# A three-block kernel whose mLSTM rows are spread over the partitions by DMA in place of picking matmuls

## The reference

```python
def mlstm_chunkwise(q, k, v, li, lf):
    ...
        m_row = jnp.maximum(inter, jnp.max(dmat, axis=-1))
        w_intra = jnp.exp(dmat - m_row[..., None])
        ...
        s_qk = jnp.einsum('bhld,bhsd->bhls', qj, kj) * w_intra
        num = jnp.einsum('bhls,bhse->bhle', s_qk, vj) + ...
        hj = num / jnp.maximum(jnp.abs(den), jnp.exp(-m_row))[..., None]
    ...
    hm = hm * jax.nn.sigmoid(heads(p['ml_o'], ML_HEADS))
    y_ml = rmsnorm(hm, ml_norm_g.reshape(ML_HEADS, ML_HD)).reshape(b, s, ML_W) * jax.nn.silu(p['ml_z'])
```

## Time and profile before

| | |
|---|---|
| median of 3 runs | 2338.71 us |
| lowest and highest run | 2337.97 and 2342.67 us |
| span of the profiled execution, first to last instruction | 2341.0 us |
| the profiled execution's own time | not given apart from the span |
| TensorE busy | 96% of the span |
| DVE, ScalarE, POOL busy | 51%, 40%, 38% |
| granted clock of TensorE, mean | 0.992 |
| DMA engines, mean busy share | 22.5% by the main queue |

### The profile page before, as it was taken

How to read it: one execution, slowest core, us unless ns; L and a number is a source line. 1 busy time by engine, 2 the same in 40 slices (tenths; PEclk the granted TensorE clock), 3 DMA queues, 4 the chain that set the end, 5 groups by cost and what they waited for, 6 DMA issues and landing times. The chain is left out here.

```text
span 2341.0 us, 38427 instructions
## 1 busy us (share of the span) xinstructions
PE 2245.5 (96%) x16046; PEld 1743.2 (74%) x16046; DVE 1193.9 (51%) x2014; ACT 947.8 (40%) x1364; POOL 898.2 (38%) x678
## 2 busy tenths in 40 slices
PE   7999999999999999999999988878999999999997
PEld 5776777787877857777788777776666778888885
DVE  5544834334245467342343878854644657317334
ACT  5423355345353324654343433324266342222243
POOL 4342343334434404333344422222333445545543
PEclk9999999999999999999999989999999999999998
DMA  4221221222222202222233200002211232232332
GB/s 159 84 85 36 73 90 64 72 73 85 98 81 81 90 22 87 81 66 79 68 106 104 72 3 4 4 19 77 72 64 57 81 105 91 99 99 91 99 99 72
DMA packets 50568, 175.18 MB, mean 75 GB/s; under 512 B 6036, under 2 KB 7004, under 8 KB 50396
## 3 DMA queue, kind: packets, MB, share of 16 engines
q1 hardware_dynamic: 50396, 172.73, 22.5%
HBM read 170.60 MB, written 2.11 MB: 74 GB/s over the span
## 5 line engine op out<-in xcount | busy, mean ns | idle before, releaser
L349 POOL TENSOR_TENSOR w_low<-work,w_high 128x512 fp32r<-128x512 f32 x622 | 835.6, 1365 | 1245.2 <-ACT w_high L298 1245.2
L279 PE MATMUL ps<-x_high_tiles,w_high 128*128 128x512 f32 x1544 | 624.9, 405 | 17.5 <-POOL w_low L349 10.9
L298 ACT ACTIVATE w_high<-work 128x1024 fp32r<-128x1024 f32 x311 | 329.2, 1059 | 733.7 <-PE ps L279 730.3
L279 PE MATMUL ps<-x_low_tiles,w_high 128*128 128x512 f32 x1544 | 604.0, 391 | 0.8 <-DVE x_low_tiles L371 0.8
L279 PE MATMUL ps<-x_high_tiles,w_low 128*128 128x512 f32 x1544 | 603.5, 391 | 0.0
L279 PE MATMUL ps<-arena_parts,w_high 128*128 128x512 f32 x1264 | 397.6, 391 | 4.3 <-DVE arena L437 1.6
L279 PEld LDWEIGHTS ps<-x_high_tiles,w_high 128*128 128x128 f32 x1544 | 291.0, 188 | 118.4 <-issue 44.5
L279 PEld LDWEIGHTS ps<-x_low_tiles,w_high 128*128 128x128 f32 x1544 | 290.9, 188 | 64.2 <-DVE x_low_tiles L371 1.6
L279 PEld LDWEIGHTS ps<-x_high_tiles,w_low 128*128 128x128 f32 x1544 | 291.4, 189 | 63.3 <-issue 6.0
L279 PEld LDWEIGHTS ps<-arena_parts,w_high 128*128 128x128 f32 x1264 | 237.3, 188 | 56.8 <-issue 3.2
L279 PE MATMUL ps<-arena_parts,w_low 128*128 128x512 f32 x608 | 236.6, 389 | 0.0
(11 more groups left out here) (452 smaller groups left out, 2864.5 us busy)
## 6 DMA issues: line engine op xcount, KB each, us to landing
work<-w_first SPq DMA_DIRECT2D x178, 512.0 KB, 3.7
work<-w_second SPq DMA_DIRECT2D x134, 512.0 KB, 3.6
xT_sb<-xT SPq DMA_DIRECT2D x8, 256.0 KB, 6.0
outT<-arena SPq DMA_DIRECT2D x8, 256.0 KB, 2.1
arena<-distance_bias SPq DMA_DIRECT2D x4, 256.0 KB
small<-small SPq DMA_DIRECT2D x1, 815.5 KB, 4.5
arena<-consts SPq DMA_DIRECT2D x1, 544.0 KB, 3.8
base<-consts SPq DMA_DIRECT2D x1, 512.0 KB
```

The source lines that it names most:

```text
L279: ins = pe.matmul(out, lhsT, rhs, start=(n == 0 and k == 0 and q == 0), stop=(n == unit["granules"] - 1 and k == len(ops[i]) - 1 and q == 2))
L298: act.activation(m.wh[:, split_of(g), :], m.raw[:, raw_of(g), :], ACT.Copy).then_inc(sem["high_ready"], 1)
L349: pool.tensor_tensor(m.wl[:, split_of(g), part], m.raw[:, raw_of(g), part], m.wh[:, split_of(g), part].bitcast(F32), ALU.subtract).then_in ...
```

## The change

The maximum's rows and the rows of the norm's factor are spread by DMA from SBUF to SBUF. The source is one row on one partition, read 128 times; the destination is a tile of 128x512 in SBUF, 256 KB.

- The maximum's four rows are issued on SP's queue (`spreads`), when `u_ready` is set, ahead of the load of one granule of the weights that the stage loads for the next stage. In layer 0 that is the first of these three granules (granule 29), in layer 1 the last. They land in four tiles of their own. `arguments` waits for the DMA of its head and reads SBUF.
- The norm's factor: ScalarE issues four DMAs directly behind the exponential, and DVE waits for each head's.
- A head's two squares are added on DVE in turn 19 + 2h, in place in the first square's tile, and TensorE sums the one tile in call 40 + 4h instead of 39 + 4h.
- `gla_side` on TensorE waits for `ml_total` instead of the last read of a spread row.

```diff
@@ product_stage, sync
+                for at, (name, value), dst, extra, landed in spreads:
+                    if at == g:
+                        sp.wait_ge(sem[name], value)
+                        sp.dma_start(dst, extra).then_inc(sem[landed], 16)
                 sp.dma_start(m.raw[:, raw_of(g), :], src).then_inc(sem[f"raw{raw_of(g)}_loaded"], 16)
@@
+def spread_of(row):
+
+    return row.rearrange("p (a n) -> p a n", a=1).broadcast_to([1, P, S])
+
+
+def row_spreads(m, at):
+
+    G = m.rows[0:ML_H, 5, :]
+    return [(at, ("u_ready", 1), m.ml_rows[h], spread_of(G[h:h + 1, :]), f"ml_row{h}_spread") for h in range(ML_H)]
@@ mlstm_side
-        def head_rows(h):
-
-            if h >= 2:
-                pe.wait_ge(sem["ml_arg_ready"], T * (h - 1))
-            pe.matmul(m.ps[:, rbank[h % 2], :], m.pick[0:ML_H, h * P:(h + 1) * P], G, start=True, stop=True).then_inc(sem["ml_rows_ready"], 1)
-
...
-        head_rows(0)
...
-            if j == 1 and h + 1 < ML_H:
-                head_rows(h + 1)
...
             if j == 0:
-                dve.wait_ge(sem["ml_rows_ready"], h + 1)
+                dve.wait_ge(sem[f"ml_row{h}_spread"], 16)
...
-            dve.tensor_scalar(a, m.ps[:, rbank[h % 2], j * P:S], m.u_tok[:, j * ML_H + h:j * ML_H + h + 1], 0.0,
+            dve.tensor_scalar(a, m.ml_rows[h][:, j * P:S], m.u_tok[:, j * ML_H + h:j * ML_H + h + 1], 0.0,
                               ALU.subtract, ALU.max).then_inc(sem["ml_arg_ready"], 1)
@@ mlstm_norm
     def tensor(pe, sem):
-        yield from turns(2 * start + 3)
+        yield from turns(2 * start + 4)
         pe.wait_ge(sem["qk_log"], 2 * DSA_H)
         for h in range(ML_H):
-            for e in range(2):
-                pe.wait_ge(sem["ml_sq"], 2 * h + e + 1)
-                ins = pe.matmul(m.ps[0:ML_H, bank, :], m.one_column[:, 3 - h:7 - h], m.ml_squares[:, e, :],
-                                start=(h + e == 0), stop=(h + e == ML_H))
-            ins.then_inc(sem["ml_sum"], 1)
+            pe.wait_ge(sem["ml_sq_added"], h + 1)
+            pe.matmul(m.ps[0:ML_H, bank, :], m.one_column[:, 3 - h:7 - h], m.ml_squares[:, 0, :], start=(h == 0),
+                      stop=(h == ML_H - 1)).then_inc(sem["ml_sum"], 1)
             yield from turns(4)
-        for h in range(ML_H):
-            pe.wait_ge(sem["ml_rstd"], 1)
-            if h:
-                pe.wait_ge(sem["ml_spread_read"], h)
-            pe.matmul(m.ps[:, bank, :], m.pick[0:ML_H, h * P:(h + 1) * P], rstd, start=True, stop=True).then_inc(sem["ml_spread"], 1)
-            yield from turns(2)
...
         act.activation(rstd, rstd, ACT.Exp, scale=-0.5).then_inc(sem["ml_rstd"], 1)
+        act.wait_ge(sem["ml_rstd"], 1)
+        for h in range(ML_H):
+            act.dma_start(m.ml_rstds[h], spread_of(rstd[h:h + 1, :])).then_inc(sem[f"ml_rstd{h}_spread"], 16)
 
     def vector(dve, sem):
-        yield from turns(start + 2 * ML_H)
+        yield from turns(start)
+        for h in range(ML_H):
+            yield
+            dve.wait_ge(sem["ml_sq"], 2 * h + 2)
+            dve.tensor_tensor(m.ml_squares[:, 0, :], m.ml_squares[:, 0, :], m.ml_squares[:, 1, :], ALU.add).then_inc(sem["ml_sq_added"], 1)
+            yield
...
-            dve.wait_ge(sem["ml_spread"], h + 1)
+            dve.wait_ge(sem[f"ml_rstd{h}_spread"], 16)
...
-                ins = dve.scalar_tensor_tensor(out=x, in0=x, scalar=g, in1=m.ps[:, bank, :], op0=ALU.mult, op1=ALU.mult)
+                ins = dve.scalar_tensor_tensor(out=x, in0=x, scalar=g, in1=m.ml_rstds[h], op0=ALU.mult, op1=ALU.mult)
@@ gla_side
-        pe.wait_ge(sem["ml_spread_read"], ML_H)
+        pe.wait_ge(sem["ml_total"], 1)
@@ build
+        spread = sb("spread", [P, 2, S])
...
+        m.ml_rows = [spread[:, 0, :], spread[:, 1, :], rs[:, 2, :], arena[:, 28, :]]
+        m.ml_rstds = [spread[:, 0, :], spread[:, 1, :], arena[:, 28, :], arena[:, 29, :]]
...
+                          spreads=row_spreads(m, granules(both + after) + len(ahead) - 1) if ahead else (),
...
+                      late=[(3, ("low_ready", 2), *load) for load in bias_in] + bounce, spreads=row_spreads(m, granules(units)))
```

More of the change, by code:

```diff
@@ L144, in later, with product_stage @@
     return Side(side.names, shift(side.tensor, 2 * granules), shift(side.scalar, granules), shift(side.vector, granules))
-def product_stage(nc, m, weights, units, splits=(), all_first=False, side=None, banks=NB, norm=None, begun=None, begun_split=NSPLIT, ahead=(), late=(), held=(), stores=(), scaled=None, arrive=(), arrivals=None, constants=()):
+def product_stage(nc, m, weights, units, splits=(), all_first=False, side=None, banks=NB, norm=None, begun=None, begun_split=NSPLIT, ahead=(), late=(), held=(), stores=(), scaled=None, arrive=(), arrivals=None, constants=(), spreads=()):
     jobs, done_at, unit_of = [], [], []
@@ L991, in mlstm_side @@
     zf, ab, lf, F, u, G = mlstm_rows(m)
-    sbank, rbank = (6, 1, 2), (7, 0)
+    sbank = (6, 1, 2)
     steps = [(h, j) for h in range(ML_H) for j in range(T)]
@@ L1106, in vector @@
                     ins.then_inc(sem["ml_sum_ready"], 1)
-    return Side(["ml_rows_ready", "ml_qk_ready", "ml_arg_ready", "ml_exp_ready", "ml_w_ready", "ml_num_done", "ml_sum_ready", "ml_sum_used",
+    return Side([*[f"ml_row{h}_spread" for h in range(ML_H)], "ml_qk_ready", "ml_arg_ready", "ml_exp_ready", "ml_w_ready", "ml_num_done", "ml_sum_ready", "ml_sum_used",
                  "ml_num_copied", "ml_dve_own"], tensor, scalar, vector)
@@ L1163, in vector @@
         dve.wait_ge(sem["ml_spread_read"], ML_H)
-    return Side(["ml_sq", "ml_sum", "ml_total", "ml_log", "ml_rstd", "ml_spread", "ml_spread_read"], tensor, scalar, vector)
+    return Side(["ml_sq", "ml_sq_added", "ml_sum", "ml_total", "ml_log", "ml_rstd", *[f"ml_rstd{h}_spread" for h in range(ML_H)], "ml_spread_read"], tensor, scalar, vector)
 def gla_side(m, banks, qkv_jobs, act_jobs):
@@ L2782, in build @@
                       norm=[small_in[0][1]], arrive=[small_in[0][0]] + [(m.xT[:, k, :], xT[k, :, :]) for k in range(KD)] + ones, arrivals=arrivals, constants=scalars,
-                      late=[(3, ("low_ready", 2), *load) for load in bias_in] + bounce)
+                      late=[(3, ("low_ready", 2), *load) for load in bias_in] + bounce, spreads=row_spreads(m, granules(units)))
         begun = len(weights)
```

## The result

| | before | after |
|---|---|---|
| median of 4 runs each | 2338.34 us | 2434.29 us |
| lowest to highest run | 2336.37 to 2342.67 | 2432.00 to 2436.47 |
| span of the profiled execution | 2341.0 us | 2431.8 us |
| mean granted clock | 0.992 | 0.973 |

The kernel became slower, by 96.0 us by these medians (4.1%); the recorded ratio is 1.0398 with an interval of 1.0385 to 1.0411, some 3 us less. That lies above the range of the prediction (to 2420).

A forecast was written before the change was run, and what follows sets the result against it. TensorE, busy 96% of the span, was taken to bound the kernel. 2341.0 - 21.1 net gain + 32.9 waits + 13.8 clock = 2366.6 us for the profiled execution, 2364 for a median; range 2346 to 2420.

The forecast's parts named there:

- What is removed: On TensorE: norm's picks 8.4 us, maximum's picks 6.3 and 0.8, eight sums of squares 7.2; together 22.7 us saved.
- The wait for the add: TensorE waits for DVE's add at granules 20, 22, 24: 5.84, 4.77, 5.84 us a layer, 32.9 us together.
- The clock: Behind each of the six add pauses TensorE's clock drops to about half: 2.3 us each, 13.8 us.
- The landing: Time for one spread row's DMA from SBUF to SBUF: between 2.1 and 10.9 us, with 2.1 taken.
- the low end: Row landing priced by a 256 KB store from SBUF: 2.1 us, the value taken for the forecast.
- The high end: Row landing if one partition gives no more than one of sixteen DMA engines draws, 24 GB/s: 10.9 us a row.
- Then everything is hidden: With quick landings, maximum's rows arrive before the loop and norm's rows before DVE uses them: no time added.
- The issues: Eight spreads issued on SP and eight on ScalarE, 0.44 us each; ScalarE's copy and exponential still narrowly in time.
- rows are slow: Rival, chance 0.32: 10.9 us a row delays layer 0 by 33 + 2, layer 1 by 6, norm 3 a layer; 2411 us.
- clock holds: Rival, chance 0.10: TensorE's clock stays up through pauses of 5 to 6 us, so 2350 us.
- no pause: Rival, chance 0.09: DVE's add is done one granule earlier, before granule 19's evacuation, leaving only the gain: 2318 us.
- picks hidden: Rival, chance 0.05: removing TensorE's picking matmuls gives nothing, while the pauses stay: 2385 us.

The follow-up runs named there:

- d2: Whole change against the kernel before, with adds a turn earlier, norm's rows issued one at a time, maximum's rows spaced on ScalarE in stage one; 2316.95 us, ratio 0.9900.
- a1: Kernel before with only the added squares, in the changed places, and nothing spread by DMA; 2383.30 us, ratio 1.0185.
- c1: Whole change with every wait and issue kept, but each spread copies a tile already on 128 partitions; 2359.16 us, ratio 1.0083 against the kernel before.
- f1: d2 with its eight spread sources replaced by ones of other partition widths, for landing times only; ran once, 2316.73 us.
- d1: Kernel before with squares added on DVE in turn 18 + 2h, summed in TensorE's call 39 + 4h, no rows by DMA; 2334.14 us, ratio 0.9970.
- e1: Kernel before with only the norm's rows by DMA, issued by ScalarE in pairs, in turns 26 and 29; 2340.70 us, ratio 0.9998.

## Why the prediction was wrong

- **What is removed, 22.7 us:** right. `d2` has nothing else in it and gains 23.6; the norm's picks gave 7.5 (8.4), the sums 6.4 (7.2).
- **The wait for the add, 32.9 us:** right, 33.1, six times, 5.79, 5.06 and 5.69 instead of 5.84, 4.77 and 5.84, and none at granule 26.
- **The clock, 13.8 us:** right for the six pauses: 14.5 by the windows behind them in the kernel after, 13.1 in `a1`. What it left out are the pauses that the slow rows make, which cost another 11 us of clock.
- **The landing: the step that failed.** "I take the low end, the only row with an SBUF source of this size": 2.1 us. Measured were 11.8 for the first row and 9.4 more for each one behind it. The new DMA reads one partition 128 times, and `c1`, which reads 128 partitions, shows that this makes the difference. The high end, 10.9 us from the share of one engine, was nearly right in size, but not for its reason: all sixteen engines were busy at 28 GB/s, and in `f1` a fifth of their time gave the same 27. That the two numbers lie close is luck. The row nearest in size was taken, not the row nearest in what limits: a wrong choice between two ends that both stood there. The Trainium skill (SBUF — State Buffer, "Door 1: The DMA port swizzle") gave 9.6 us a row, and the trace has 9.4.
- **"Then everything is hidden":** wrong with it. Layer 0 waited 24.9 us and lost some 2 of clock (the rival said 33 and 2), layer 1 waited 3.2 (6).
- **The issues, "0.44 each … both hold, narrowly":** wrong, and wrong in the rival as well. The rival "rows are slow" had the mechanism right but gave the norm 3 us a layer, for DVE. That was nothing: DVE waited 8.2 us for a row in all, and TensorE not for that. What it missed was that the third and fourth issue last 6.8 and 9.6 us when the rows ahead are slow. ScalarE stood 17.8 us, its copy of weights was late, and TensorE lost 17.4 us in layer 0 (13.69 + 3.68) and about as much in layer 1. With this term in place of the 6 us the rival's 2411 would be 2440; with its layer 0 and layer 1 terms at the measured 24.9 and 3.2 it would be 2429, beside 2434 measured. The top of the range, 2420, rested on the rival without this term, and so the result lies above it.
- **The other rivals** (clock holds, no pause, picks hidden) did not occur. `d2` speaks against hidden picks. The mechanism of "no pause" was real a turn earlier: that is `d1`.

What stays open is what exactly holds an issue. It is not the number of DMAs in flight alone: in `c1` two are in flight at the third issue too, with as many packets each (144 in both kernels), and it takes 0.6 us. How much undone work it takes wasn't measured. Open too are the landings of the narrow sources for which the trace has none.

## What to carry to other kernels

Price a DMA by its slowest side: a copy that reads one partition 128 times went at 27 to 28 GB/s, four neighbouring partitions no faster, sixteen spread ones in 3 us. Such a row was free where nobody needed it for 12 us, no other row was in flight, and the weights could land some 9 us late; four in one go blocked the engine that issued them and the weights on the other queue, so space them a transfer apart and never put them ahead of an engine's urgent work. And when a wait is put on the busiest engine, look which turn the awaited operation stands in: one turn on DVE was worth some 50 us here.

## What the runs showed that was not expected

- **An issue can hold its engine.** With two slow rows in flight the third took 6.8 us and the fourth 9.6, on SP and on ScalarE alike; with quick ones (`c1`) 0.6, on SP up to 1.4. Behind slow rows even SP's next issue of a load of weights took up to 9.6. The Trainium skill (DMA: Bandwidth & Descriptors, "Issuing engines are not separate DMA queues") says that the issue's time is usually small beside the DMA; the trace disagrees for this pattern, where the issue is 6.8 of the 29.9 us to landing and 9.6 of 32.1.
- **Slow rows on one queue slow the other queue.** Weights issued by SP landed in 3.7 us at the median, and in `e1`, where the rows are on ScalarE's queue, in up to 24.6. The same section says that all DMAs run on the same sixteen engines; the trace agrees, with a busy share of 0.9 at 28 GB/s while rows are read.
- **The width of a source in neighbouring partitions says little:** 0 to 15 in 4.5 to 5.4 us, sixteen spread ones in 3.1 to 3.2.
